# Up-projection matmuls of a three-layer float32 transformer: high and low activations side by side in 512-column matmuls

## The reference, cut to what matters

```python
D_MODEL = 1024; SEQ = 256; D_FF = 2816        # layers 0 and 1; the third layer's MLP is 4096 wide

def conv_ffn(h, w_up, conv_w, conv_b, w_down):        # layers 0 and 1
    S = h.shape[1]
    u = h @ w_up                                      # 1024 -> 2 x 2816
    pad = CONV_WIDTH // 2                             # CONV_WIDTH = 3
    up = jnp.pad(u, ((0, 0), (pad, pad), (0, 0)))
    u = sum(up[:, t:t + S] * conv_w[t] for t in range(CONV_WIDTH)) + conv_b
    gate, val = jnp.split(u, 2, axis=-1)
    return (jax.nn.silu(gate) * val) @ w_down
```

## Time and profile before

| what | value |
| --- | --- |
| median of 3 runs | 1076.44 us (1075.25 to 1076.63) |
| the profiled execution, its own time | 1077.12 us |
| its span, first to last instruction | 1075.4 us |
| TensorE busy (matmuls) | 1058.1 us, 98% |
| VectorE busy | 728.9 us, 68% |
| ScalarE busy | 589.2 us, 55% |
| weight and input traffic | 175.6 MB read, 164 GB/s over the span |

### The profile page before, as it was taken

The page is one execution under the profiler, slowest core; times in us unless marked ns, Lnnn a source line. Parts: engine busy times, 40 slices in busy tenths (PEclk is TensorE's granted clock), DMA queues, the critical chain, the costliest instruction groups (busy, mean ns, idle before and its releaser), DMA issues.

```text
span 1075.4 us, 17488 instructions
## 1 busy us (share of the span) xinstructions
PE 1058.1 (98%) x6920; PEld 956.3 (89%) x6920; DVE 728.9 (68%) x997; ACT 589.2 (55%) x893; POOL 92.1 (9%) x150
## 2 busy tenths in 40 slices
PE   8899999999999999999999999999999999999997
PEld 7788899999998887899999998899899989998996
DVE  5976677877777855477787777866655586555553
ACT  5766765555546757565564556734433566434442
POOL 1311110000000243210000000401000000000000
PEclk9999999999999999999999999999999999999999
DMA  8633345566554441345555545564353356565531
GB/s 292 221 120 128 118 157 175 181 228 199 158 194 152 162 144 53 118 159 174 194 197 195 196 157 186 176 189 156 115 160 121 123 179 215 167 198 192 186 126 40
DMA packets 114644, 177.51 MB, mean 165 GB/s; under 512 B 3419, under 2 KB 85524, under 8 KB 114580
## 3 DMA queue, kind: packets, MB, share of 16 engines
q1 hardware_dynamic: 114004, 175.05, 49.3%
q10 hardware_dynamic: 576, 1.57, 0.4%
HBM read 175.56 MB, written 1.05 MB: 164 GB/s over the span
## 4 chain that ended last, share of the span: by engine, by line
PE 89%; ACT 5%; SPq 2%; issue 2%; DVE 1%; POOL 1%; DMA 1%; POOLq 0%; ACTq 0%; DVEq 0%
PE ps L1803 85%; PE ps L1877 1%; DMA raw<-in_diff_w_qkv 1%; ACT whi L682 1%; ACT scr L854 1%; ACT whi L670 1%; POOL scr L575 1%; PE ps L1923 1%; PE ps L2046 1%; PE ps L2268 0%; PE ps L2391 0%; SPq L436 0%; ACT scr L706 0%; ACT scr L1084 0%; ACT scr L908 0%
## 5 line engine op out<-in xcount | busy, mean ns | idle before, releaser
L1190 DVE TENSOR_TENSOR wlo<-raw,whi 128x2048 fp32r<-128x2048 f32 x149 | 341.3, 2296 | 79.7 <-ACT whi L670 78.3
L1803 PE MATMUL ps<-xhi,whi 128*128 128x256 f32 x1248 | 355.2, 285 | 0.0
L1803 PE MATMUL ps<-xlo,whi 128*128 128x256 f32 x1248 | 353.1, 283 | 0.0
L1803 PE MATMUL ps<-xhi,wlo 128*128 128x256 f32 x1248 | 353.1, 283 | 0.0
L670 ACT ACTIVATE whi<-raw 128x2048 fp32r<-128x2048 f32 x149 | 282.8, 1909 | 53.1 <-PE ps L1803 34.3
L1803 PEld LDWEIGHTS ps<-xhi,whi 128*128 128x128 f32 x1248 | 239.2, 192 | 3.9 <-issue 1.4
L1803 PEld LDWEIGHTS ps<-xlo,whi 128*128 128x128 f32 x1248 | 239.3, 192 | 1.2
L1803 PEld LDWEIGHTS ps<-xhi,wlo 128*128 128x128 f32 x1248 | 239.3, 192 | 0.0
L806 ACT ACTIVATE scr<-scr,cwT 128x256 f32<-128x256 f32 x88 | 48.1, 594 | 142.3 <-DVE scr L1333 142.3
L1803 PE MATMUL ps<-whi,ohi 128*128 128x512 f32 x368 | 124.8, 397 | 0.0
L1803 PE MATMUL ps<-whi,olo 128*128 128x512 f32 x368 | 122.2, 390 | 0.0
(11 more groups left out here) (188 smaller groups left out, 1141.2 us busy)
## 6 DMA issues: line engine op xcount, KB each, us to landing
raw<-in_ffn_w_up SPq DMA_DIRECT2D x44, 1024.0 KB, 5.1
raw<-in_w_in SPq DMA_DIRECT2D x23, 1024.0 KB, 5.3
raw<-in_ffn_w_down SPq DMA_DIRECT2D x22, 1024.0 KB, 5.0
raw<-in_w_mlp_in SPq DMA_DIRECT2D x16, 1024.0 KB, 5.3
raw<-in_w_mlp_out SPq DMA_DIRECT2D x16, 1024.0 KB, 4.9
raw<-in_diff_w_qkv SPq DMA_DIRECT2D x11, 1024.0 KB, 6.3
raw<-in_ple_w_gate SPq DMA_DIRECT2D x8, 1024.0 KB, 4.9
raw<-in_swa_w_qkv SPq DMA_DIRECT2D x6, 1024.0 KB, 5.5
```

The costliest lines, as they stand in the source:

```text
L1190: dve.tensor_tensor(wlo[:, u % RING, :], raw[:, u % RAW, :], whi[:, u % RING, :].bitcast(F32), ALU.subtract).then_inc(lo_ready, 1)
L1803: return pe.matmul(o, l, r, start=start, stop=stop, skip_group_check=True)
```

## The change

x_hi and x_lo, two tensors before, become one, `xs[P, 8, 2, 256]`: for each k the 256 columns of x_hi and the 256 of x_lo are neighbours. A matmul with w_hi can now take both as 512 moving columns. It writes w_hi·x_hi to the first half of a bank and w_hi·x_lo to the second; w_lo·x_hi is added to the second half. So each tile m has a bank of its own, a unit has two, and the result is the sum of the two halves of a bank. The matmuls of a unit are grouped: all high ones of both tiles, then all low ones; in the value unit the low ones come first. TensorE has a new wait before each FFN up unit, for the sums of the same kind of unit one iteration back (`summed`), since gate units always use banks 4 and 5 and value units banks 6 and 7.

Added for each up unit: a ScalarE copy of the second halves from PSUM to `ulow` (or `rel`), and a VectorE add of that to the first halves. In the FFN the `rB` product then reads the sum, and `sums` stands ahead of `keep_ahead` in VectorE's order. In the MLP, VectorE does the ReLU and the square in one instruction, and ScalarE makes the high half as a copy of it.

```diff
-        xhi = sb("xhi", [P, KD, SEQ], F32R)
-        xlo = sb("xlo", [P, KD, SEQ], F32R)
+        xs = sb("xs", [P, KD, 2, SEQ], F32R)
+        xhi, xlo = xs[:, :, 0, :], xs[:, :, 1, :]
...
+                    def low(gv, used):
+
+                        act.wait_ge(weights_used, used)
+                        act.activation(ulow[:, gv, :].rearrange("p (j c) -> p j c", j=2),
+                                       ps[:, 4 + 2 * gv:6 + 2 * gv, SEQ:2 * SEQ], ACT.Copy).then_inc(low_read[l], 1)
...
                         for gv in range(2):
                             keep_ahead(ug + gv, i)
+                            low(gv, at(ug + gv + 1, TURN, i))
                             mid(it, gv, buf, i)
...
                     ahead(u0)
+                    low(0, u0 + 1)
                     rms_row(l)
                     preload(2 * l, ACT.Silu)
                     mid(0, 0, 0)
                     ahead(u0 + 1)
+                    low(1, u0 + 2)
                     mid(0, 1, 0)
...
-                    act.activation(rel[:, b, :], ps[:, 4 + b, :], ACT.Relu).then_inc(relu_ready, 1)
-                    act.wait_ge(relu_ready, at(it + 1, MLP_TURN, i))
-                    act.activation(ohi[:, 2 * b:2 * b + 2, :].rearrange("p a c -> p (a c)"), rel[:, b, :], ACT.Square)\
+                    bank = 4 + 2 * (it % 2)
+                    act.activation(rel[:, b, :].rearrange("p (j c) -> p j c", j=2), ps[:, bank:bank + 2, SEQ:2 * SEQ],
+                                   ACT.Copy).then_inc(rlow_read, 1)
+                    act.wait_ge(sq_ready, at(it + 1, MLP_TURN, i))
+                    act.activation(ohi[:, 2 * b:2 * b + 2, :].rearrange("p a c -> p (a c)"), rsq[:, b, :], ACT.Copy)\
...
+                    def sums(it, gv, i=None):
+
+                        scaled_up = usc[:, it % 2, gv, :].rearrange("p (j c) -> p j c", j=2)
+                        dve.wait_ge(low_read[l], at(2 * it + gv + 1, 2 * FFN_TURN, i))
+                        dve.tensor_tensor(scaled_up, ps[:, 4 + 2 * gv:6 + 2 * gv, 0:SEQ],
+                                          ulow[:, gv, :].rearrange("p (j c) -> p j c", j=2), ALU.add).then_inc(summed[l], 1)
+                        if it == 0 and gv == 0:
+                            dve.wait_ge(rB_ready, l + 1)
+                        dve.wait_ge(summed[l], at(2 * it + gv + 1, 2 * FFN_TURN, i))
+                        dve.tensor_tensor(scaled_up, scaled_up, rB[:, :].unsqueeze(1).broadcast_to([P, 2, SEQ]),
+                                          ALU.mult).then_inc(scaled[l], 1)
...
                         for gv in range(2):
+                            sums(it, gv, i)
                             keep_ahead(ug + gv, i)
-                            taps(it, gv, i, ug)
+                            taps(it, gv, i)
...
-                    dve.tensor_tensor(rsq[:, b, :], rel[:, b, :], rel[:, b, :], ALU.mult).then_inc(sq_ready, 1)
+                    dve.tensor_tensor(up, ps[:, bank:bank + 2, 0:SEQ], up, ALU.add).then_inc(rsum_ready, 1)
+                    dve.wait_ge(rsum_ready, n)
+                    dve.scalar_tensor_tensor(rsq[:, b, :], rel[:, b, :], 0.0, rel[:, b, :], ALU.max, ALU.mult)\
+                        .then_inc(sq_ready, 1)
...
+                def up_high(u, m, bank, part, start, xwait=None):
+                    wh = slot(whi, u, KD)
+                    for k in part:
+                        if xwait is not None:
+                            pe.wait_ge(xlo_ready, xwait + KD + max(k + 1, 2))
+                        ins = mm(ps[:, bank + m, :], wh[:, k, m * P:(m + 1) * P], xs[:, k, :, :].rearrange("p a c -> p (a c)"),
+                                 start and k == 0, False)
+                    return ins
+
+                def up_low(u, m, bank, start):
+                    wl = slot(wlo, u, KD)
+                    for k in range(KD):
+                        ins = mm(ps[:, bank + m, SEQ:2 * SEQ], wl[:, k, m * P:(m + 1) * P], xhi[:, k, :], start and k == 0, False)
+                    return ins
...
-                    fm_half(u, 0, xhi, xlo, KD, 4, 2 * KD * n, part=range(0, 4))
+                    pe.wait_ge(*unit_split(u))
+                    up_high(u, 0, 4, range(0, 4), True, 2 * KD * n)
                     norm_T(n, 1, 1)
-                    fm_half(u + 1, 0, xhi, xlo, KD, 5, part=range(0, 4))
-                    fm_half(u, 0, xhi, xlo, KD, 4, 2 * KD * n, part=range(4, KD))
-                    fm_half(u, 1, xhi, xlo, KD, 4)
-                    fm_half(u + 1, 0, xhi, xlo, KD, 5, part=range(4, KD))
-                    if between:
-                        between()
-                    fm_half(u + 1, 1, xhi, xlo, KD, 5)
+                    up_high(u, 1, 4, range(0, 4), True)
+                    up_high(u, 0, 4, range(4, KD), False, 2 * KD * n)
+                    up_high(u, 1, 4, range(4, KD), False)
+                    up_low(u, 0, 4, False)
+                    up_low(u, 1, 4, False).then_inc(weights_used, 1)
+                    up_unit(u + 1, 6, True, None, between)
...
-                    def up(ug, buf, gv, i=None):
-
-                        for m in range(2):
-                            fm_half(ug, m, xhi, xlo, KD, 4 + 2 * buf + gv, None, i)
+                    def up(ug, it, gv, i=None):
+
+                        pe.wait_ge(summed[l], at(2 * (it - 1) + gv + 1, 2 * FFN_TURN, i))
+                        up_unit(ug, 4 + 2 * gv, gv == 1, i)
```

More of the change, by code:

```diff
@@ L210, in three_layer_kernel @@
         usc = region(4096, 2048, "p (b g c) -> p b g c", b=2, g=2)
+        ulow = region(7168, 1024, "p (g c) -> p g c", g=2)
         ga = pp[:, :, :].rearrange("p t (m c) -> p (t m) c", c=SEQ)
@@ L304, in three_layer_kernel @@
         mid_ready = [sem(f"mid_ready{l}") for l in range(2)]
+        low_read = [sem(f"low_read{l}") for l in range(2)]
+        summed = [sem(f"summed{l}") for l in range(2)]
         scaled = [sem(f"scaled{l}") for l in range(2)]
@@ L318, in three_layer_kernel @@
         mlo_ready = sem("mlo_ready")
-        relu_ready = sem("relu_ready")
+        rlow_read = sem("rlow_read")
+        rsum_ready = sem("rsum_ready")
         sq_ready = sem("sq_ready")
@@ L1117, in _ @@
                     act.wait_ge(merged, j + 1)
-                    act.activation(xhi[:, 2 * j:2 * j + 2, :].rearrange("p a c -> p (a c)"), mB[:, j, :], ACT.Copy)\
+                    act.activation(xhi[:, 2 * j:2 * j + 2, :], mB[:, j, :].rearrange("p (a c) -> p a c", c=SEQ), ACT.Copy)\
                         .then_inc(mhi_ready, 1)
@@ L1325, in ffn, with taps @@
                     u0 = U0[f"ffn{l}"]
-                    def taps(it, gv, i=None, ug=None):
-                        buf = it % 2
[L1330 to L1335, removed]
+                    def sums(it, gv, i=None):
[8 more added lines that the diff above has]
+                                          ALU.mult).then_inc(scaled[l], 1)
+                    def taps(it, gv, i=None):
+                        buf = it % 2
                         dve.wait_ge(mid_ready[l], at(2 * it + gv + 1, 2 * FFN_TURN, i))
@@ L1375, in ffn @@
                     ahead(u0)
-                    dve.wait_ge(rB_ready, l + 1)
+                    sums(0, 0)
                     taps(0, 0)
+                    sums(0, 1)
                     ahead(u0 + 1)
@@ L1850, in fm_half, with up_unit @@
                         ins.then_inc(signal, 1)
+                def up_high(u, m, bank, part, start, xwait=None):
[11 more added lines that the diff above has]
+                    return ins
+                def up_unit(u, bank, low_first, i=None, between=None):
+                    pe.wait_ge(*unit_split(u, i))
+                    if low_first:
+                        for m in range(2):
+                            up_low(u, m, bank, True)
+                        for m in range(2):
+                            if between and m:
+                                between()
+                            ins = up_high(u, m, bank, range(KD), False)
+                    else:
+                        for m in range(2):
+                            up_high(u, m, bank, range(KD), True)
+                        for m in range(2):
+                            ins = up_low(u, m, bank, False)
+                    ins.then_inc(weights_used, 1)
                 def row_piece(u, t, b, hi, lo, kk, bank, c0, w, start, stop, k0=0, signal=None, by=1):
@@ L2166, in iteration @@
                         for gv in range(2):
-                            up(ug + gv, it % 2, gv, i)
+                            up(ug + gv, it, gv, i)
                         down(ug + 2, it - 1, False, False, i)
@@ L2179, in ffn @@
                         for gv in range(2):
-                            up(u0 + 26 + 2 * n + gv, it % 2, gv)
+                            up(u0 + 26 + 2 * n + gv, it, gv)
                     down(u0 + 30, 8, False, False)
@@ L2452, in mlp_up @@
                 def mlp_up(u, it, i=None):
-                    for m in range(2):
```

(2 more changed lines are left out.)

8 lines of the change are left out of this document (5 added, 3 removed).

## The result

The changed kernel takes 1067.80 us (median of 5 runs, 1065.54 to 1069.17), the kernel before, timed beside it, 1076.56 us (5 runs, 1075.25 to 1077.38). The ratio is 0.9917 [0.9905, 0.9928]: faster by 0.8%. Timed again, beside three variants, it was 1066.24 us against 1076.48, ratio 0.9904 [0.9887, 0.992]. The profiled execution took 1065.9 us, its span 1064.2.

A forecast was written before the change was run, and what follows sets the result against it. TensorE, busy 98% of the span, was taken as the bound. Joined matmuls save 11.2 us behind the heads and 0.5 in them, 11.7 in all; the median of 1076.44 us becomes 1064.7, range 1063.5 to 1067.8.

The forecast's parts named there:

- price 0.227: Up units: a joined 512-column matmul costs 0.227 us between starts, as in the steady down unit, against 0.240 for two narrow.
- The rivals at 0.232 and 0.240: Up units: joined matmuls cost more, giving 1069.5 us (chance 0.05) or 1076.4, with 1074 if partly saved (chance 0.04).
- waits 0.23, and 0.03 more at each following piece: Stage heads: TensorE's wait for the last quarter's low x, taken as 0.25 us, leaving 0.17 us gained per head.
- TensorE has 4 matmuls (0.91 us): Stage heads: TensorE's work behind the transposes before it needs the last quarter's low x, where it had 12 matmuls.
- 8.9 behind the last up unit: FFN end: VectorE has the last hidden value 8.9 us after the last up unit; needed at 9.6, margin 0.7 us.
- about 1.3: FFN end: time after the last gate unit until ScalarE is at the copy, the first term of VectorE's 14.4 us chain.
- I forecast no wait: FFN end: TensorE would not wait for the last hidden value, with a margin of 0.7 us.
- the heads don't hold: FFN ends: margins of 0.3, 0.5 and 0.7 us overrun by some 1.5 us each; up to 1067.8 us, chance 0.10.
- VectorE's period: FFN loop: VectorE's own iteration falls from 15.51 to 14.15 us, 2.4 below TensorE's 16.56.
- The slower rival: FFN loop: waits for the middle tap stay, VectorE's period becomes 18.2 us and the kernel takes 1090 us; chance 0.05.
- The change of width costs no extra time: Up units: the order of high and low matmuls only sets how often width changes; value units low first count 0.

The follow-up runs named there:

- unjoined: Changed kernel with each joined matmul issued as two of 256 columns, banks, copies, sums and waits kept: 1078.42 us, ratio 1.0025 to the kernel before.
- head_cover: Changed kernel with low-weight matmuls of k 0 to 3 moved ahead of those needing the last low x in the three heads: 1065.50 us, ratio 0.9898.
- end_late_split: Changed kernel with the weight split at each FFN's end moved from behind the second residual add to behind the fourth: 1065.90 us, ratio 0.9898.
- extra_two: Changed kernel with two dead VectorE multiplies of 512 columns before every FFN sum: 1092.46 us, ratio 1.0158 to the kernel before.
- alternate: Changed kernel with joined and low matmuls taking turns for each k, in all units except each stage's first: 1072.67 us, ratio 0.9964.
- head_and_end: Changed kernel with both low-weight matmuls moved forward in the heads and the FFN-end weight split moved behind the fourth residual add: 1064.73 us, ratio 0.9888.
- extra_op: Changed kernel with one dead VectorE multiply of 512 columns before every FFN sum: 1071.45 us, ratio 0.9954 to the kernel before.

## Why the prediction was right

It said 1064.7 us, 1063.5 to 1067.8; the median is 1067.8 and, timed again, 1066.2. So the first median lies on the very edge of the range, an edge that came from a rival with chance 0.10; that it is not outside is in part luck. The direction and the mechanism were right. Behind the start the sum promised 11.7 us and 9.7 came. The rest of the distance is within the spread of the runs (1065.54 to 1069.17); most of that probably is the start, which the traces show to vary, but of the five runs behind this median only one has a trace.

- **The price 0.227 was right.** The earlier trace rows priced the joined matmul before it existed: 16 of them take 3.63 us. The rivals at 0.232 and 0.240 are out. The loops gained 4.13 us each, against 4.16, and unjoined puts the join at 12.9 ns a pair in them. The rule of the Trainium skill ("TensorE: Matmul & The Clock Gate", section "Back-to-back issue gap") gives 2.5 ns a pair; the runs don't bear it out for this stream. The prediction left out that the section states this rule for an isolated matmul; for a stream in which each matmul has its weight load it gives some 131 ns at 512 columns, and the 227 ns here don't agree with that either.
- **The heads were mis-sized.** The step "waits 0.23, and 0.03 more at each following piece" named the right wait and place. For four pieces its own terms add up to 0.32, but the sum took 0.25; head_cover measured 0.33. The step "TensorE has 4 matmuls (0.91 us)" took the steady price; around the transposes four took 1.02 and 1.01. Before the change the twelve at the same places were over their steady price too (1.50 and 1.51 instead of 1.44), so only part of that is new: over a whole FFN head it is 0.35 us against 0.20, and the four transposes take 0.41 us instead of 0.36. So each FFN head lost 0.11 us instead of gaining 0.17.
- **The end was the step that failed.** The prediction found the tight place, "8.9 behind the last up unit", margin 0.7; it was 9.4, margin 0.1, chiefly because the low half of iteration 9 came 1.9 us after the gate unit, not "about 1.3". That still brought no stall to speak of (0.1 us), as forecast. But the text stopped there: "I forecast no wait" looked at the last hidden value and not at what VectorE has queued behind it. The split at 323.65 and the third add behind it came late, a term that the sum has at nothing, and it cost 0.62 us per FFN; end_late_split gave it back. The rival "the heads don't hold" allowed 1.5 us in each FFN for overrun margins of 0.3, 0.5 and 0.7 us. None of these was overrun by more than the 0.1 us; the 1.24 us of the ends came at a hand-over that the rival didn't name, and the 0.56 us of the heads from mis-sized terms. That its upper edge held the result is luck, too.
- **VectorE's period was right** (14.11 against 14.15) and with it the claim that a copy and an add per unit are free in the loops: the loops of unjoined are 172.59 us, those of before too. The slower rival, VectorE as the bound, needs two more operations per unit (extra_two), not none.
- **"The change of width costs no extra time"** holds for this order and for groups of two but for 0.03 us at a step from narrow to wide, which the earlier trace rows did show as the dearer first six of a down unit. It does not hold where the width changes at every matmul (alternate, 6 ns a pair); no row of before could tell that.

## What to carry to other kernels

A matmul's price is the distance between starts, and a steady stretch of the wanted shape elsewhere in the same trace prices a merge of two matmuls to a nanosecond; the fixed part saved per merged pair was 13 ns here where TensorE never waits. When an added operation is "hidden", follow the hiding engine's queue past the last hand-over that you checked: lateness that it builds up where its cover is thin can fall due at a later hand-over (here the third residual add), and moving one independent piece of work behind that hand-over gave it back. Tenths of a microsecond are told by distances between marked instructions in two traces, not by medians.

## What the runs showed of the hardware

- **The start varies.** The first up matmul of FFN 0 began anywhere between 141.79 and 145.37 us in the twelve traces (before 143.87, changed 142.20). The shifts arise in the first 43 us and stay within 0.1 us from there to the FFN; their cause is not shown. In two traces part of the shift is a slower clock: granted 0.75 from 10 to 15 us in end_late_split, after TensorE had stood 3.1 us, and 0.70 from 40 to 45 us in head_and_end, after TensorE had been busy for 2.9 of the 5 us before. The changed kernel has 1.00 in both windows. The profiles before and after differ there by 1.67 us, which a subtraction of their times (11.2 us) would credit to the change.
- **The order of widths matters only at the finest grain**: 353 ns for a wide and a narrow one in turn, 348 in groups of two, 347 in groups of sixteen.
- **A stall of 5.6 us drew a slower clock after it** (extra_two): granted clock 0.50 for some 5 us. After the stall of 1.9 us in extra_op the granted clock stayed at the upper level; its first two matmuls stand 0.34 and 0.24 us before the next ones, and steady ones follow.
